# Two more projection blocks cut into token halves at three norm transitions of a two-layer trunk, with their weights split ahead

## The chip, the cores and the metric

One core of a Trainium2 chip (trn2) runs the whole step in one launch. The time is the device time of that launch in microseconds (us). A core has five engines that run beside each other, each with a queue of its own worked off in order, and that wait for one another through semaphores only: PE (TensorE, matmuls), DVE (VectorE), ACT (ScalarE), POOL (GpSimd) and SP (SyncE, which here issues the DMAs). PE writes to PSUM, eight banks of 512 floats on 128 partitions, and ACT and DVE read its results there.

## The reference

The trunk has two layers over 128 context tokens and 512 latent tokens, 1024 features wide. Each layer is a mixer and a gated convolutional FFN; each of the four sub-layers is wrapped in two norms. What lies between two sub-layers is this:

```
def rmsnorm(x, g):
    xf = x.astype(jnp.float32)
    y = xf * lax.rsqrt(jnp.mean(xf * xf, axis=-1, keepdims=True) + EPS)
    return (y * g.astype(jnp.float32)).astype(x.dtype)
...
    h = rmsnorm(x, prm["norm_pre"][l, 0]) * (1.0 + scale1) + shift1
    (mixer: projections of h, attention and/or delta rule, then @ w_out -> mix)
    x = x + gate1 * rmsnorm(mix, prm["norm_post"][l, 0])
    h = rmsnorm(x, prm["norm_pre"][l, 1]) * (1.0 + scale2) + shift2
    f = conv_ffn(h, prm["ffn_w_up"][l], prm["ffn_conv"][l], prm["ffn_w_down"][l])
    x = x + gate2 * rmsnorm(f, prm["norm_post"][l, 1])
...
def conv_ffn(h, w_up, conv_w, w_down):
    u = dwconv_centred(h @ w_up, conv_w)
    a, b = jnp.split(u, 2, axis=-1)
    return (jax.nn.silu(a) * b) @ w_down
```

Layer 0 has the even mixer (attention and delta rule), layer 1 the odd one: `h @ w_in` gives 384 query columns (`cq`), 256 key-value columns (`ckv`) and 64 rotary columns (`kpe`); `cq` and `ckv` are normed again and projected into heads.

## The kernel before

**Tiling.** All activations lie transposed, features on the partitions, as eight chunks of 128 features (`KD` = 8) by 644 token columns (`TW`: 640 tokens and gaps). The columns are cut into two halves of 322 (`HW`, function `tk(g)`). A projection is done in blocks of 128 output columns, numbered through the whole program; `n` is the number, `N0_FFN[l]`, `N0_ODD_IN` and so on are the first of a stage. To reach full precision each operand is split in two fp32r numbers, hi and lo, and a product is three matmuls (hi·hi, hi·lo, lo·hi). A block of eight chunks is thus 8 x 3 x 2 halves = 48 matmuls of 128x322.

**Weights.** SP loads block n into `w_raw[n % 2]` when the lo part of block n-2 is written (`raw_free`). ACT copies it to `w_hi` (`hi`, L782), DVE subtracts to get `w_lo` (`w_rest`, L1338). Both have two buffers. The guard of `hi(n)` before the copy is

```
                if not isinstance(n, int) or n >= 2:
                    act.wait_ge(proj_done, n - 1)
```

and `proj_done` counts finished blocks, so that block n-2 has been read. The output projections have six further weight buffers, `RESH` and `RESL` (named `w_out_hi`, `w_out_lo`), which lie in the space of `g_hi` and `g_lo` and hold output blocks 2 to 7.

**A norm transition.** There are three of them with the same code: i = 0 (even output projection into the up projection of layer 0), i = 1 (down projection of layer 0 into the odd layer's input projection), i = 2 (odd output projection into the up projection of layer 1). While PE still works on half 1 of the projection in front of the norm, ACT and DVE already norm half 0. PE's part is `pair_halves`:

1. half 0 of the first two blocks, n and n+1 (`pair_chunk`, L1997), with the statistics of the norm behind (`post_stat`) among them;
2. `second_stat` (L2034): eight fp32 matmuls of ones with squares of x, which sum them over the features of half 1; each pair waits for a square on ACT (L853);
3. half 1 of blocks n and n+1, chunk by chunk, as `h_lo` of half 1 comes (L1413 on DVE, behind L874 on ACT, L1407 on DVE, and the root on ACT, L841 and L843);
4. then the remaining blocks by `proj` (L1964), both halves at a time.

On ACT and DVE `second_half` is the other side of this: root of the norm behind, four pairs of x (`x_pair`, L1371 and L1373), four squares, root of the norm in front, eight chunks of h. For i = 1 PE also turns the context rows there, and ACT copies them from PSUM (`context`).

**After it.** In the FFN, blocks come in pairs, a and b. For each pair ACT and DVE run a `body`: ACT splits the weights two blocks ahead, evacuates PSUM into `u` and `conv` (L1168, L1169) for a, then the same for b, then silu (L1172), and `g_hi` (L1174); DVE does the lo part, two convolution steps per block (L1797, L1800), the gating (L1808) and `g_lo` (L1810). There are 11 bodies per half of the FFN; the middle ones are a hardware loop. A block uses PSUM banks 0 and 1 or 2 and 3, by n % 2. Banks 4 to 7 are used by the statistics alone. In the odd layer six blocks follow: ACT evacuates three `cq`, two `ckv` and one `kpe` block; PE does the statistic of `cq` (`norm_stat`, L1985) behind block 3 and that of `ckv` behind block 5; the first head projections follow. POOL zeroes the edge columns of `g_hi` and `g_lo`.

## Time and profile before

| | us |
|---|---|
| median of 3 runs | 1990.46 |
| lowest and highest | 1989.63, 1992.21 |
| the profiled execution, its time | 1988.44 |
| its span, first to last instruction | 1986.6 |
| PE busy | 1869.2 (94%) |
| DVE busy, ACT busy | 964.9 (49%), 845.1 (43%) |
| PE's share of the chain that ended last | 86% |
| TensorE clock, mean | 0.982 of full |

The profile is of one execution. Matmuls overlap, so one that is listed with 0.31 us may be issued 0.15 us after the one before it; what counts is the distance of their starts. The fp32 statistics matmuls appear as two records each. The idle time of an engine stands in brackets behind the row that ended it, with what released it. The granted clock is given as a share of 2.4 GHz.

### The profile page before, as it was taken

Reading aid. Unit: us, or ns where it says so; the run is one execution under the profiler, and the core shown is the slowest. Engines: PE = TensorE matmul, PEld = TensorE weight load, DVE = VectorE, ACT = ScalarE, POOL = GpSimd, SP = SyncE. Lnnn points to the kernel's source line nnn. Section 1 sums busy time; section 2 is a strip of 40 time slices with the busy share of each in tenths; the row PEclk is TensorE's granted clock in tenths of the full one; section 3 lists DMA queues with packets and bytes.
Section 4 is the critical chain, followed back from the end, with each engine's and each line's share of the span. In section 5 each row is a group of like instructions: output and inputs, shape, how many; then the busy total and the mean of one; then the engine's idle time right before and its main releaser. Section 6 shows DMA issues by size and latency. Waiting matters only on the chain.

```text
span 1986.6 us, 35678 instructions
## 1 busy us (share of the span) xinstructions
PE 1869.2 (94%) x14484; PEld 1725.9 (87%) x14484; DVE 964.9 (49%) x1558; ACT 845.1 (43%) x1464; POOL 87.9 (4%) x126
## 2 busy tenths in 40 slices
PE   4999999998889999999999999998899999999997
PEld 2999877776779899999999887776798999999997
DVE  4433354445655555325555754344355553255555
ACT  4445322223655544214445644343455442144453
POOL 0000233321000000000000000000000000000000
PEclk8999999999989999999999999999999999999999
DMA  7222454443020122312224311101201223122243
GB/s 276 64 66 57 175 176 168 158 167 115 1 65 25 53 74 78 88 57 74 74 86 132 101 38 48 28 25 43 64 22 56 72 78 88 57 74 74 86 132 112
DMA packets 238715, 170.12 MB, mean 86 GB/s; under 512 B 20138, under 2 KB 230284, under 8 KB 232332
## 3 DMA queue, kind: packets, MB, share of 16 engines
q1 hardware_dynamic: 238604, 168.54, 27.6%
q8 instruction: 82, 1.34, 0.3%
q14 instruction: 29, 0.24, 0.0%
HBM read 165.08 MB, written 3.44 MB: 85 GB/s over the span
## 4 chain that ended last, share of the span: by engine, by line
PE 86%; DVE 5%; ACT 4%; issue 3%; POOL 2%; DMA 0%; SPq 0%; ACTq 0%; DVEq 0%; POOLq 0%
PE ps L1964 48%; PE ps L2040 12%; PE ps L1997 5%; PE ps L2295 4%; PE ps L2145 2%; PE ps L2553 2%; PE ps L2150 2%; PE ps L2590 2%; PE ps L2549 2%; POOL level_b L730 1%; PE ps L2430 1%; PE ps L2407 1%; ACT w_hi L782 1%; PE ps L1985 1%; DVE scores L1762 1%
## 5 line engine op out<-in xcount | busy, mean ns | idle before, releaser
L782 ACT ACTIVATE w_hi<-w_raw 128x1024 fp32r<-128x1024 f32 (+4 forms) x193 | 205.1, 1063 | 580.4 <-PE ps L1964 478.7
L1338 DVE TENSOR_TENSOR w_lo<-w_raw,w_hi 128x1024 fp32r<-128x1024 f32 (+4 forms) x197 | 241.5, 1227 | 394.2 <-ACT w_hi L782 394.0
L1964 PE MATMUL ps<-h_hi,w_hi 128*128 128x322 f32 x1744 | 403.6, 313 | 5.3 <-ACT conv L1169 2.4
L1964 PE MATMUL ps<-h_lo,w_hi 128*128 128x322 f32 x1744 | 402.4, 312 | 0.0
L1964 PE MATMUL ps<-h_hi,w_lo 128*128 128x322 f32 x1744 | 400.1, 310 | 0.0
L1964 PEld LDWEIGHTS ps<-h_hi,w_hi 128*128 128x128 f32 x1744 | 294.2, 189 | 7.2 <-DVE w_lo L1338 3.4
L1964 PEld LDWEIGHTS ps<-h_hi,w_lo 128*128 128x128 f32 x1744 | 295.4, 189 | 0.0
L1964 PEld LDWEIGHTS ps<-h_lo,w_hi 128*128 128x128 f32 x1744 | 295.3, 189 | 0.0
L2040 PE MATMUL ps<-g_hi,w_hi 128*128 128x322 f32 x352 | 110.8, 315 | 2.7 <-DVE g_lo L1810 1.6
L2040 PE MATMUL ps<-g_hi,w_lo 128*128 128x322 f32 x352 | 109.3, 311 | 0.0
L2040 PE MATMUL ps<-g_lo,w_hi 128*128 128x322 f32 x352 | 109.2, 310 | 0.0
L1797 DVE SCALAR_TENSOR_TENSOR conv<-u,vec_cols,conv 128x642 f32<-128x642 f32 x88 | 78.0, 886 | 12.5 <-ACT conv L1169 12.1
L1800 DVE SCALAR_TENSOR_TENSOR conv<-u,vec_cols,conv 128x642 f32<-128x642 f32 x88 | 78.1, 887 | 11.1 <-DVE conv L1797 0.6
L1174 ACT ACTIVATE g_hi<-gated 128x642 f32 (+1 forms) x44 | 32.6, 741 | 104.5 <-DVE gated L1808 104.5
L1014 ACT ACTIVATE level_z<-ps 128x256 f32<-128x256 f32 (+1 forms) x60 | 22.9, 382 | 110.8 <-PE ps L2295 93.8
L2040 PEld LDWEIGHTS ps<-g_hi,w_hi 128*128 128x128 f32 x352 | 66.3, 188 | 4.0 <-DVE g_lo L1810 2.2
L1169 ACT ACTIVATE conv<-ps,vec_cols 128x644 f32<-128x644 f32 x88 | 69.7, 792 | 0.0
L2040 PEld LDWEIGHTS ps<-g_lo,w_hi 128*128 128x128 f32 x352 | 66.4, 189 | 0.2
L2040 PEld LDWEIGHTS ps<-g_hi,w_lo 128*128 128x128 f32 x352 | 66.4, 189 | 0.0
L1824 DVE COPY f_t<-ps 128x644 f32 (+1 forms) x16 | 13.3, 828 | 100.9 <-PE ps L1964 82.3
L1964 PE MATMUL ps<-g_hi,w_lo 128*128 128x322 f32 x264 | 60.8, 312 | 0.0
L1168 ACT ACTIVATE u<-ps 128x644 f32<-128x644 f32 x88 | 60.8, 691 | 0.0
(367 smaller groups left out, 3372.8 us busy)
## 6 DMA issues: line engine op xcount, KB each, us to landing
w_raw<-in_ffn_w_up SPq DMA_DIRECT2D x88, 512.0 KB, 3.6
w_mod_raw<-in_w_mod SPq DMA_DIRECT2D x40, 1024.0 KB, 5.0
w_raw<-in_ffn_w_down SPq DMA_DIRECT2D x48, 704.0 KB, 4.3
w_raw<-in_ev_w_in SPq DMA_DIRECT2D x18, 512.0 KB, 3.6
w_mod_first<-in_w_mod SPq DMA_DIRECT2D x8, 1024.0 KB, 15.7
w_raw<-in_ev_w_out SPq DMA_DIRECT2D x8, 512.0 KB, 3.9
w_raw<-in_od_w_out SPq DMA_DIRECT2D x8, 512.0 KB, 3.8
w_raw<-in_od_w_kv_up SPq DMA_DIRECT2D x24, 128.0 KB, 2.2
```

Of the source, the lines that this page charges most:

```text
L782: act.activation(WH[slot][:, 0:k, :], RAW[slot][:, 0:k, :], ACT.Copy).then_inc(w_hi, 1)
L1168: act.activation(halves(U[b][:, :]), pair(2 * slot), ACT.Copy).then_inc(S("f_u"), 1)
L1169: act.activation(halves(Y[b][:, :]), pair(2 * slot), ACT.Copy, scale=vcol(v0 + b * FCH, j)).then_inc(evac_a, 1)
L1338: dve.tensor_tensor(WL[slot][:, 0:k, :], RAW[slot][:, 0:k, :], WH[slot][:, 0:k, :].bitcast(F32), ALU.subtract).then_inc(w_lo, 1)
L1797: dve.scalar_tensor_tensor(y[:, 1:643], u[:, 0:642], vcol(v0 + b * FCH, j), y[:, 1:643], ALU.mult, ALU.add).then_inc(S(f"f_conv{b}"), 1)
L1800: last = dve.scalar_tensor_tensor(y[:, 1:643], u[:, 2:644], vcol(v0 + b * FCH + 4 * FCH, j), y[:, 1:643], ALU.mult, ALU.add)
L1964: last = pe.matmul(out, w_of(k, wi), x_of(k, xi, i), start=(k == 0 and p == 0), stop=(k == ks - 1 and p == 2))
L1997: last = pe.matmul(bank(2 * slot + hf, HW), (WH, WL)[wi][slot][:, k, :], x[xi][:, k, hf * HW:(hf + 1) * HW], start=(k == 0 and p == 0), st ...
L2040: last = pe.matmul(out, w[wi][:, k, :], x[xi][:, k, tk(g)], start=(k == 0 and p == 0), stop=(k == ks - 1 and p == 2))
L2145: return pe.transpose(out, src, IDENT[0:rows, 0:rows])
L2150: last = pe.matmul(PS[32 * j:32 * j + 32, b * 512:b * 512 + 512], SCX[:, k, :], w[:, 512 * j:512 * j + 512], start=(k == 0), stop=(k == KD ...
L2295: last = pe.matmul(out(b, h), w[half(b), h, :], x(b, h), start=True, stop=True)
```

## The change

At each of the three transitions blocks n+2 and n+3 are now treated like n and n+1, with half 0 before half 1:

- **PE.** Behind `second_stat` comes `second_pair(0)`: half 0 of blocks n+2 and n+3. Behind half 1 of n and n+1 comes `second_pair(1)`: their half 1. Their results go to banks 4 to 7. The loop over the up blocks begins at block 6, with blocks 4 and 5 written out in front of it.
- **Weights.** Blocks n+2 and n+3 are split into `RESH`/`RESL` buffers instead of `w_hi`/`w_lo`: the copy on ACT (`ahead_hi`) behind the root of the norm behind and behind the second square, the subtraction on DVE behind the last `x_pair`. `next_weights` gives the buffers; `res_slot` turns round which output block uses which, so that these two are free in time.
- **Bodies.** In body 0 the weights of blocks n+4 and n+5 are split (`ahead` = 4), by the same `hi` with its guard unchanged; body 1 splits none and reads banks 4 to 7. In the odd layer blocks 0 and 1 split blocks 4 and 5, blocks 2 and 3 none, and the `cq` statistic stands behind block 4, in banks 6 and 7.
- **Edges.** POOL zeroes the edges of `g_hi` and `g_lo` when block n+3 is done, and PE waits for it only in front of the down blocks.

```
+    def res_slot(m):
+
+        return (m + 2) % 6
+
+    def next_weights(i, u):
+
+        x = u + (1 if i % 2 else 2)
+        return RESH[x], RESL[x]
...
-                pool.wait_ge(S("half_done"), 8 * (l + 1))
+                pool.wait_ge(proj_done, N0_FFN[l] + 4)
...
+            def ahead_hi(i, u):
+
+                n = N0_OUT[i] + (2 * KD if i % 2 else KD) + u
+                act.wait_ge(w_landed[n % 2], landed_by(n))
+                if i % 2:
+                    act.wait_ge(proj_done, N0_OUT[i] + 2 * KD)
+                else:
+                    act.wait_ge(S("half_done"), 8 * (i // 2) + 4)
+                act.activation(next_weights(i, u)[0][:, :, :], RAW[n % 2][:, 0:KD, :], ACT.Copy).then_inc(w_hi, 1)
+
             def second_half(i, between=None):
 
                 root(i, "post", 1)
+                ahead_hi(i, 2)
                 for j in range(4):
                     x_square(i, 1, j)
-                    if between and j == 1:
-                        between()
+                    if j == 1:
+                        if between:
+                            between()
+                        ahead_hi(i, 3)
                 root(i, "pre", 1)
...
-                    def body(j, ks):
+                    def body(j, ks, ahead=2, b0=0):
                         c = c0 + j
                         for b in range(2):
                             n = n0 + b + 2 * j
                             slot = (n0 + b) % 2
                             act.wait_ge(proj_done, n + 1)
-                            hi(n + 2, slot=slot, k=ks, landed=landed_by(n0 + b + 2) + 16 * j)
+                            if ahead:
+                                hi(n + ahead, slot=slot, k=ks, landed=landed_by(n0 + b + ahead) + 16 * j)
...
-                    body(0, KD)
-                    with act.Fori(1, FH - 1) as j:
+                    if half == 0:
+                        body(0, KD, 4)
+                        body(1, KD, 0, 4)
+                    else:
+                        body(0, KD)
+                    with act.Fori(2 - half, FH - 1) as j:
...
-                hi(n + 2)
+                if m not in (2, 3):
+                    hi(n + (4 if m < 2 else 2))
...
(DVE, second_half, behind the four x_pair)
+                for u in (2, 3):
+                    n = N0_OUT[i] + (2 * KD if i % 2 else KD) + u
+                    w = next_weights(i, u)
+                    dve.wait_ge(w_hi, n + 1)
+                    dve.tensor_tensor(w[1][:, :, :], RAW[n % 2][:, 0:KD, :], w[0][:, :, :].bitcast(F32), ALU.subtract).then_inc(w_lo, 1)
...
(PE, pair_halves)
                 second_stat(i)
+                if between:
+                    pe.wait_ge(S("c_ctx"), 2)
+
+                def second_pair(g):
+
+                    for u in (2, 3):
+                        pe.wait_ge(w_lo, n + u + 1)
+                        for k in range(KD):
+                            last = half_mm(bank(4 + 2 * ((n + u) % 2) + g, HW), next_weights(i, u), (Hh, Hl), k, g, KD)
+                        if g:
+                            last.then_inc(proj_done, 1)
+                second_pair(0)
...
                 for k in range(KD - 2, KD):
                     pair_chunk(n, 1, k, (Hh, Hl), KD, (1,))
+                second_pair(1)
...
                         pair_halves(n0, 2 * l)
-                        pe.wait_ge(*filled(f"g_edges{l}"))
-                    with pe.Fori(1 - half, FH) as j:
+                        for b in range(2):
+                            proj(n0 + b + 4, H, free=[evacuated(n0 + b)])
+                    with pe.Fori(3 * (1 - half), FH) as j:
...
+                    pe.wait_ge(*filled(f"g_edges{l}"))
                     down_pair(n1, FH * (2 * l + half))
...
-            for m in range(2, 6):
-                proj(N0_ODD_IN + m, H)
-                if m == 3:
-                    norm_stat("cq")
+            for m in range(4, 6):
+                proj(N0_ODD_IN + m, H, free=[evacuated(N0_ODD_IN + m - 4)])
+                if m == 4:
+                    norm_stat("cq", 6)
```

The order of instructions shows it at three places of the first transition. In brackets stand the semaphores an instruction waits for.

PE, from the last two statistics matmuls on, before: half 1 of block 0 with `w_hi1`, chunk by chunk behind `h_lo`.

```order
L2034 MATMUL ps<-x_sq1_85,consts_61 128x322 [waits x_squared]
L2034 MATMUL ps<-x_sq1_85,consts_61 128x322
L1997 MATMUL ps<-h_hi_50,w_hi1_58 128x322 [waits h_lo,half_evacuated]
L1997 MATMUL ps<-h_lo_51,w_hi1_58 128x322
L1997 MATMUL ps<-h_hi_50,w_lo1_60 128x322
L1997 MATMUL ps<-h_hi_50,w_hi1_58 128x322 [waits h_lo]
```

And after: half 0 of block 2, with weights from an output buffer (`w_out_hi4`), waits for its own weights alone.

```order
L2071 MATMUL ps<-x_sq1_85,consts_61 128x322 [waits x_squared]
L2071 MATMUL ps<-x_sq1_85,consts_61 128x322
L2077 MATMUL ps<-h_hi_50,w_out_hi4_98 128x322 [waits w_lo_written]
L2077 MATMUL ps<-h_lo_51,w_out_hi4_98 128x322
L2077 MATMUL ps<-h_hi_50,w_out_lo4_104 128x322
L2077 MATMUL ps<-h_hi_50,w_out_hi4_98 128x322
```

48 such matmuls, with `w_out_hi4` and then `w_out_hi5`, have come between the statistics and the first wait for `h_lo` of half 1.

ACT, from the root of the norm behind (`post_rstd`) to that of the norm in front (`pre_rstd`), before:

```order
L843 ACTIVATE post_rstd_93<-post_rstd_93 128x322 [waits norm_root]
L853 ACTIVATE x_sq0_84<-x_t_49 128x644 [waits x_added]
L853 ACTIVATE x_sq1_85<-x_t_49 128x644 [waits x_added]
L853 ACTIVATE x_sq0_84<-x_t_49 128x644 [waits x_stat,x_added]
L853 ACTIVATE x_sq1_85<-x_t_49 128x644 [waits x_stat,x_added]
L841 ACTIVATE pre_rstd_92<-ps,eps_73 128x322 [waits h_scaled,x_stat]
```

And after:

```order
L852 ACTIVATE post_rstd_93<-post_rstd_93 128x322 [waits norm_root]
L894 ACTIVATE w_out_hi4_98<-w_raw1_56 128x1024 [waits half_done,w_landed1]
L862 ACTIVATE x_sq0_84<-x_t_49 128x644 [waits x_added]
L862 ACTIVATE x_sq1_85<-x_t_49 128x644 [waits x_added]
L894 ACTIVATE w_out_hi5_99<-w_raw0_55 128x1024 [waits half_done,w_landed0]
L862 ACTIVATE x_sq0_84<-x_t_49 128x644 [waits x_stat,x_added]
L862 ACTIVATE x_sq1_85<-x_t_49 128x644 [waits x_stat,x_added]
L850 ACTIVATE pre_rstd_92<-ps,eps_73 128x322 [waits h_scaled,x_stat]
```

One weight copy has come in front of the first square and one in front of the third.

ACT, from the silu of body 0 to the first weight copy in the loop, before (that copy is for block 4):

```order
L1172 ACTIVATE silu_a_116<-conv0_114 128x642 [waits f_conv0]
L1174 ACTIVATE g_hi_52<-gated_117 128x642 [waits f_gated]
L1177 UNCONDITIONAL_BRANCH
L1177 ISA
L779 ISA [waits proj_done]
L782 ACTIVATE w_hi1_58<-w_raw1_56 128x1024 [waits proj_done,w_landed1]
```

And after (the copy is for block 6):

```order
L1195 ACTIVATE silu_a_116<-conv0_114 128x642 [waits f_conv0]
L1197 ACTIVATE g_hi_52<-gated_117 128x642 [waits f_gated]
L1191 ACTIVATE u0_112<-ps 128x644 [waits f_silu,f_gated,f_conv0,proj_done]
L1192 ACTIVATE conv0_114<-ps,vec_cols_62 128x644
L1191 ACTIVATE u1_113<-ps 128x644 [waits f_silu,f_gated,f_conv1,proj_done]
L1192 ACTIVATE conv1_115<-ps,vec_cols_62 128x644
L1195 ACTIVATE silu_a_116<-conv0_114 128x642 [waits f_conv0]
L1197 ACTIVATE g_hi_52<-gated_117 128x642 [waits f_gated]
L1204 UNCONDITIONAL_BRANCH
L1204 ISA
L788 ISA [waits proj_done]
L791 ACTIVATE w_hi1_58<-w_raw1_56 128x1024 [waits proj_done,w_landed1]
```

Body 1, four evacuations, a silu and a `g_hi`, now stands in front of the loop and has no weight copies.

## Rows read from the trace of the kernel before

**Rows 1.** The page: busy time by engine; a weight load (KB, us to landing).

```profile
PE 1869.2 (94%) x14484; PEld 1725.9 (87%) x14484; DVE 964.9 (49%) x1558; ACT 845.1 (43%) x1464; POOL 87.9 (4%) x126
...
w_raw<-in_ffn_w_up SPq DMA_DIRECT2D x88, 512.0 KB, 3.6
```

**Rows 2.** Timeline of PE, first transition: start us, us, operation, count, [idle before <-releaser].

```profile
643.54 4.88 PE L2034 MATMUL ps<-x_sq,consts 128*128 128x322 f32 x16
...
651.41 0.61 PE L1997 MATMUL ps<-h_hi,w_hi 128*128 128x322 f32 x1 [2.98 <-DVE h_lo L1413]
...
657.34 0.31 PE L1997 MATMUL ps<-h_hi,w_hi 128*128 128x322 f32 x1
...
661.23 0.31 PE L1997 MATMUL ps<-h_hi,w_lo 128*128 128x322 f32 x1
662.77 0.56 PE L1964 MATMUL ps<-h_hi,w_hi 128*128 128x322 f32 x2 [1.23 <-ACT conv L1169]
...
691.49 0.46 PE L1964 MATMUL ps<-h_hi,w_hi 128*128 128x322 f32 x2
```

**Rows 3.** PE by stretches, first transition: stretch, us, busy (count), PEclk, DMA share, GB/s.

```profile
648.00:649.00 1.00, 0.42 (x2) 1.00 0.00 0
...
651.00:652.00 1.00, 0.59 (x2) 0.50 0.00 0
```

**Rows 4.** Timeline of ACT, from the first transition's statistics into the up blocks.

```profile
641.47 0.74 ACT L853 ACTIVATE x_sq<-x_t 128x644 f32<-128x644 f32 x1 [1.76 <-DVE x_t L1373]
...
644.88 0.74 ACT L853 ACTIVATE x_sq<-x_t 128x644 f32<-128x644 f32 x1 [1.06 <-PE ps L2034]
...
662.54 1.06 ACT L782 ACTIVATE w_hi<-w_raw 128x1024 fp32r<-128x1024 f32 x1
...
668.32 0.74 ACT L1174 ACTIVATE g_hi<-gated 128x642 fp32r<-128x642 f32 x1 [1.38 <-DVE gated L1808]
...
677.50 1.06 ACT L782 ACTIVATE w_hi<-w_raw 128x1024 fp32r<-128x1024 f32 x1 [4.82 <-PE ps L1964]
...
679.05 0.79 ACT L1169 ACTIVATE conv<-ps,vec_cols 128x644 f32<-128x644 f32 x1
...
682.91 0.74 ACT L1174 ACTIVATE g_hi<-gated 128x642 f32 x1 [2.44 <-DVE gated L1808]
```

**Rows 5.** Timeline of DVE, same stretch.

```profile
645.42 0.83 DVE L1373 TENSOR_TENSOR x_t<-x_t,f_t 128x644 f32<-128x644 f32 x1
649.53 1.01 DVE L1407 SCALAR_TENSOR_TENSOR h_chunk<-x_t,pre_gain,pre_rstd 128x320 f32<-128x320 f32 x2 [3.28 <-ACT pre_rstd L843]
...
656.97 0.55 DVE L1413 SCALAR_TENSOR_TENSOR h_lo<-h_chunk,mod,h_hi 128x320 fp32r<-128x320 f32 x1 [0.16 <-ACT h_hi L874]
```

**Rows 6.** Timeline of PE, transition into the odd layer.

```profile
1140.30 1.35 PE L2034 MATMUL ps<-x_sq,consts 128*128 128x322 f32 x4 [0.25 <-ACT x_sq L853]
...
1169.56 1.25 PE L1985 MATMUL ps<-sq_sum,consts 128*128 128x322 f32 x4
...
1184.94 1.25 PE L1985 MATMUL ps<-sq_sum,consts 128*128 128x322 f32 x4
1185.78 0.71 PE L1964 MATMUL ps<-cq_hi,w_hi 128*128 128x322 f32 x2
```

**Rows 7.** Odd layer: DVE at 1128.66 and 1180.47, ACT at 1175.51 and 1178.06.

```profile
1128.66 1.23 DVE L1338 TENSOR_TENSOR w_lo<-w_raw,w_hi 128x1024 fp32r<-128x1024 f32 x1 [1.27 <-ACT w_hi L782]
...
1175.51 0.74 ACT L1243 ACTIVATE cq_hi<-cq 128x644 fp32r<-128x644 f32 x1
1178.06 0.53 ACT L782 ACTIVATE w_hi<-w_raw 128x384 fp32r<-128x384 f32 x1 [1.80 <-PE ps L1964]
...
1180.47 0.83 DVE L1349 TENSOR_TENSOR sq_sum<-sq_sum,sq 128x644 f32<-128x644 f32 x1
```

**Rows 8.** Timeline of PE, third transition.

```profile
1487.48 4.89 PE L2034 MATMUL ps<-x_sq,consts 128*128 128x322 f32 x16
...
1506.34 0.56 PE L1964 MATMUL ps<-h_hi,w_hi 128*128 128x322 f32 x2 [1.22 <-ACT conv L1169]
```

44 lines of the change are left out of this document (24 added, 20 removed).

## The prediction

> **What bounds the kernel now.** I read the page first, then the timelines of PE, ACT and DVE around the three places where a norm lies between two projections. PE is busy for 94% of the span [rows 1], so a gain can only come from a stretch in which PE stands idle or runs at the lower clock. The transitions are such stretches. Take the first, into the up projections of layer 0. Eight statistics matmuls (16 records) start at 643.54 and the last one leaves PE at about 648.25 (the run of 4.88 us less what the last matmul overlaps, 0.17). Then PE is idle for 2.98 us until the first `h_lo` chunk of token half 1 [rows 2]. The granted clock, still 1.00 (2.4 GHz) at 648 to 649, is 0.50 (1.2 GHz) at 651 to 652 [rows 3], so the 22 matmuls between 651.41 and 657.34 come every 0.27 us. From 657.34 they come at full rate, and the pair of blocks is issued at 661.38 (one step after the row at 661.23). Then PE waits again, until 662.77, for ACT's evacuation and the split of the next weights. Full rate is read from 662.77 to 691.49: four blocks of 48 matmuls in 28.72 us, 0.150 us each, **7.18 us a block** [rows 2]. In the rest I number the blocks after the norm 0 to 6; 691.49 is the start of block 6.
>
> **Part 1: matmuls that move.** PE now runs half 0 of blocks 2 and 3 (48 matmuls, 7.2 us) between the statistics and half 1 of blocks 0 and 1, and their half 1 behind it. No matmul is added: 48 and 48 take the place of 96. Each of them keeps one weight load, as before (matmuls and loads have equal counts in [rows 1]). What the move covers at the first transition: idle 651.41 - 648.25 = 3.16 us; half 1 of blocks 0 and 1 took 661.38 - 651.41 = 9.97 us where 7.18 is enough, 2.79 us of low clock and of waits for chunks; the gap 662.77 - 661.38 = 1.39 us, since block 2's weights and banks are now ready ahead. Sum 7.3 us. Half 1 now starts at 648.25 + 0.25 + 7.18 = 655.7 (0.25 us is a guess for the first matmul behind statistics). The first `h_lo` chunk is there at 651.3 and the eighth at 657.5 [rows 2, 5], 0.9 us apart; PE wants the eighth only at 655.7 + 0.45 x 2 + 0.9 x 5 = 661.1, and each earlier one late enough too. No wait there.
>
> **Part 2: weight splits that move.** Two ACT copies and two DVE subtractions per transition go ahead, in the order shown above. ACT's first copy (1.06 us, the price of the row at 662.54) falls into the 1.76 us in which ACT waits for DVE before the first square, at 641.47. The second stands in front of the third square, which began at 644.88 after 1.06 us of idleness: a copy of 1.06 us just fits [rows 4]. Cost 0 for both. DVE's two subtractions (1.23 us each [rows 7]) start when its last `x_t` is done, 646.25, and end at 648.7; its next work starts at 649.53 after 3.28 us of idleness [rows 5]. PE needs the first at 648.25 (done 647.5) and the second at 651.9. Cost 0, with 0.8 us to spare on DVE. If that cover were gone, half 1 would still have 655.7 - 651.3 = 4.4 us before PE noticed. In the odd layer ACT also copies the context there, and the copy delays the third square by some 0.5 us; PE sees 0.1 us of it. The weights of the second copy can only be loaded after the split that ends at 1129.89 [rows 7]; they are needed 7.5 us later, and such a load lands 3.6 us after its issue [rows 1]. The four edge memsets on POOL now wait for block 3, and PE's wait for them stands 140 us later, in front of the down blocks: cost 0.
>
> **Part 3: what is late next.** The split of block 4 keeps its old guard, `proj_done >= n - 1`, and that now means that block 2 is done, though block 4 only overwrites the buffer of block 0. Behind this copy in ACT's queue stand the evacuations of blocks 0 and 1 and both bodies of the gated convolution. By PE's count: blocks 0 and 1 end at 662.9, block 2 at 666.5, block 3 at 670.1, block 4 at 677.2, block 5 at 684.4. ACT starts the copy for block 4 at 666.5 and has evacuated block 0 2.34 us later (677.50 to 679.84 [rows 4]), 668.9, so block 4 (from 670.1) does not wait. The copy for block 5 starts at 670.1. Before, body 0 took 6.5 us from that copy to the end of `g_hi` (662.54 to 669.06); I take 6.2, since DVE is less behind: 676.3. Body 1 has no copies: two evacuations of 1.37 us, and 3.8 us from the last evacuation to `g_hi` (679.84 to 683.65), and 0.4 us because two blocks' convolutions now fall together on DVE: 683.2. Only then comes the copy for block 6, inside the loop, at 683.3, and 2.34 us later, with semaphores 685.8, PE may start block 6, which it wants at 684.4. **A new wait of 1.4 us.** Its bounds are 0 (body 1 a quarter faster) and 2.7 us (1.28 us more for entering the loop, the idle time of ACT at that place before, which hides it). The loop cannot stay late: ACT needs 2.34 + 6.15 (677.50 to 683.65) = 8.5 us a body, and PE 14.4.
>
> Gain at the **first transition**: before, 648.25 to 691.49 = 43.24 us; after, 0.25 + 5 x 7.18 + 1.4 = 37.55; **5.7 us**. At the **third** the statistics start 843.94 us later and block 2 843.57 us later [rows 2, 8], so before loses 0.37 us less: **5.3 us**.
>
> **Odd layer.** Before, the statistics leave PE at 1141.5 and the first query projection starts at 1185.78: 44.3 us. After: 0.1 + 0.25 + five blocks 35.9 + the `cq` statistic 0.84 (1184.94 to 1185.78 is the price [rows 6]) = PE stands at the `ckv` statistic at 1178.6. The `cq` statistic itself hardly moves: it stood at 1169.56, two blocks before the end, and will stand at 1170.4, one block before the end. The chain behind it ends with `cq_hi` at 1176.25 [rows 7]; I shift it by 0.4 us, between 0 (ACT was late then) and 0.84. Behind it follow the copy, the evacuation, two squares and their sum, 1178.06 to 1181.30 = 3.24 us [rows 7], which before fitted under block 5. Now they end at 1176.65 + 3.24 = 1179.9. PE waits 1.3 us, and the query projection starts at 1180.8. Gain **5.0 us**, not the 6.3 that the moved blocks save.
>
> **Sum.** 5.7 + 5.0 + 5.3 = 16.0 us. The profiled execution took 1988.44 us, so 1972.4; the median of the three runs is 2.02 us above it, 1990.46, so **1974.5 us**, 0.8% less. About 0.2%, 4 us, is what a measurement of this kernel can tell from no change.
>
> **Rival 1: the clock falls all the same.** PE no longer idles for 3 us, but in the statistics it still waits for squares in short gaps (0.25 us in [rows 6]; in the first transition PE's 4.88 us for eight matmuls hold some too), and then come dense matmuls. If the clock falls at each transition for as many matmuls as before, it costs 22 x (0.27 - 0.15) = 2.6 us each, 7.9 in all: 1982.4 us. Against it: at 648 to 649, with the statistics just over, the clock is 1.00 [rows 3], and it is lower only where PE has been idle. The Trainium skill, "TensorE: Matmul & The Clock Gate", section "A second HAM failure mode: psum-queue depth-cycling", speaks for the rival: short idle spells between groups of matmuls can be enough to make the clock swing between its two levels. By that rule the time would be the 1982.4 above; this trace does not show it. Chance 8%.
>
> **Rival 2: the waits of part 3 are larger.** Each at its upper end (2.7, 2.7, and 2.6 if body and sums run late by another 1.3), gain 12.1 us: 1978.4. Chance 13%. **Rival 3: they vanish**, gain 20.1: 1970.4. Chance 8%; it needs ACT and DVE both to run their chains faster than the rows show.
>
> **Rival 4: slower.** The up loops stay one body late. This decides where ACT's chain of a body passes PE's 14.4 us: each us above costs 9 bodies x 2 loops = 18 us, so 15.5 us a body would give 1974.5 + 20 = 1994. At 8.5 us a body it is far off; the second copy waiting for its weights decides likewise only from 7.5 + 4.4 us of loading. Chance 2%. **Rival 5: nothing moves**, because the second pair waits for its splits on PE until the chunks are there anyway (DVE 3 us late at every transition): PE would be idle as before, and keep only the gap, 1.39 x 3 less the new waits of 4.1: 1990. Chance 3%.
>
> **Chances.** Forecast 66% (gain 13 to 19), rivals 8, 13, 8, 2 and 3%. The range runs from rival 3 to rival 1, 1970 to 1982, and leaves out some 15%. Faster by over 0.2%: 94%; within: 3%; slower: 3%.
>
> **What would show it.** On PE: at 648.3 `w_out_hi` matmuls of half 0 directly behind the statistics, no idle time for `h_lo`, PEclk 1.00 through all three transitions; a new wait of 1 to 2 us for block 6 at two places, released by ACT's evacuation or DVE's `w_lo`, and one for `sq_sum` of about 1.3 us in front of the `ckv` statistic. On ACT: the copy for block 4 begins when block 2 ends. I am wrong if the clock is below 1.00 behind the statistics, if half 1 waits for chunks, or if a wait for `w_lo` stands in front of the second pair.

## The result, and the profile after

The changed kernel takes 1973.95 us (median of four runs, 1970.57 to 1978.02), the kernel before 1991.34 us in the same comparison (four runs, 1989.63 to 1994.39): a ratio of 0.9912, with a 95% interval of 0.9889 to 0.9935. It is **17.4 us faster**; 16.0 were forecast, and the forecast time was 1974.5 us. The profiled execution took 1974.58 us with a span of 1972.8, against 1988.44 and 1986.6 before.

The first transition on TensorE (PE), the answer to [rows 2]: start us, us, engine, line, operation, shapes, count, and in brackets the idle time before it and what ended it.

```profile
645.52 4.91 PE L2071 MATMUL ps<-x_sq,consts 128*128 128x322 f32 x16
650.03 0.55 PE L2077 MATMUL ps<-h_hi,w_out_hi 128*128 128x322 f32 x1
650.42 0.31 PE L2077 MATMUL ps<-h_lo,w_out_hi 128*128 128x322 f32 x1
...
657.39 0.31 PE L2034 MATMUL ps<-h_hi,w_hi 128*128 128x322 f32 x1
...
671.73 0.47 PE L2001 MATMUL ps<-h_hi,w_hi 128*128 128x322 f32 x2
...
685.73 0.46 PE L2001 MATMUL ps<-h_hi,w_lo 128*128 128x322 f32 x2
686.94 0.56 PE L2001 MATMUL ps<-h_hi,w_hi 128*128 128x322 f32 x2 [0.75 <-ACT conv L1192]
```

The `w_out_hi` matmuls are the first halves of blocks 2 and 3. They stand where 2.98 us of idle time stood; 657.39 is the start of half 1, 671.73 of block 4, 686.94 of block 6. Neither half 1 nor block 4 has a bracket: nothing waits for `h_lo` or for a weight split. Block 6 could have started one step (0.29 us) behind the row at 685.73, at 686.02, so the new wait is 0.92 us. From the first statistics matmul to block 6 it is 686.94 - 645.52 = 41.42 us, against 691.49 - 643.54 = 47.95 before [rows 2]: **6.53 us less**.

The granted clock in stretches of 1 us, the answer to [rows 3] (stretch, us, busy time and matmuls, then PE's clock as a share of 2.4 GHz, DMA share, GB/s). The first two rows stand in the first transition, the last two behind the statistics of the others:

```profile
651.00:652.00 1.00, 1.00 (x9) 1.00 1.00 284
657.00:658.00 1.00, 1.00 (x9) 1.00 0.08 16
```

```profile
1144.00:1145.00 1.00, 1.00 (x9) 1.00 0.00 0
...
1490.00:1491.00 1.00, 1.00 (x9) 1.00 0.00 0
```

ScalarE (ACT) in the same stretch, the answer to [rows 4]: both weight copies, the third square directly behind the second of them, the copies for blocks 4 and 5 (668.42 and 672.01), the end of body 0 (677.30) and of body 1 (683.85), and the copy for block 6 (684.49).

```profile
641.62 1.05 ACT L894 ACTIVATE w_out_hi<-w_raw 128x1024 fp32r<-128x1024 f32 x1
...
645.72 1.04 ACT L894 ACTIVATE w_out_hi<-w_raw 128x1024 fp32r<-128x1024 f32 x1
646.86 0.74 ACT L862 ACTIVATE x_sq<-x_t 128x644 f32<-128x644 f32 x1
...
668.42 1.06 ACT L791 ACTIVATE w_hi<-w_raw 128x1024 fp32r<-128x1024 f32 x1 [9.45 <-PE ps L2077]
...
672.01 1.06 ACT L791 ACTIVATE w_hi<-w_raw 128x1024 fp32r<-128x1024 f32 x1 [1.24 <-PE ps L2077]
...
677.30 0.74 ACT L1197 ACTIVATE g_hi<-gated 128x642 fp32r<-128x642 f32 x1 [0.90 <-DVE gated L1842]
...
683.85 0.74 ACT L1197 ACTIVATE g_hi<-gated 128x642 fp32r<-128x642 f32 x1 [1.90 <-DVE gated L1842]
684.49 1.05 ACT L791 ACTIVATE w_hi<-w_raw 128x1024 fp32r<-128x1024 f32 x1
```

VectorE (DVE), the answer to [rows 5]. The two subtractions (2.35 us together) have shrunk the idle time in front of the first chunk of half 1 from 3.28 to 1.02 us:

```profile
648.17 2.35 DVE L1434 TENSOR_TENSOR w_out_lo<-w_raw,w_out_hi 128x1024 fp32r<-128x1024 f32 x2
651.54 1.01 DVE L1440 SCALAR_TENSOR_TENSOR h_chunk<-x_t,pre_gain,pre_rstd 128x320 f32<-128x320 f32 x2 [1.02 <-ACT pre_rstd L852]
```

PE in the odd layer and at the third transition, the answers to [rows 6] and [rows 8]:

```profile
1133.85 4.82 PE L2071 MATMUL ps<-x_sq,consts 128*128 128x322 f32 x16
...
1176.58 1.35 PE L2022 MATMUL ps<-sq_sum,consts 128*128 128x322 f32 x4 [1.11 <-DVE sq_sum L1377]
1177.53 0.71 PE L2001 MATMUL ps<-cq_hi,w_hi 128*128 128x322 f32 x2
...
1479.22 4.90 PE L2071 MATMUL ps<-x_sq,consts 128*128 128x322 f32 x16
...
1520.64 0.56 PE L2001 MATMUL ps<-h_hi,w_hi 128*128 128x322 f32 x2 [0.74 <-ACT conv L1192]
```

From the statistics to the query projection it is 43.68 us (49.33 before), a gain of 5.65; at the third transition 41.42 us (47.57 before, block 6 at 1535.05), a gain of 6.15. **The three gains add up to 18.3 us**; compared like with like it is 18.0, as the next experiment shows. The spans differ by 13.8 us and the medians by 17.4, so the whole has to be read with care. The first statistics matmul of the first transition comes at 645.52 us in this profile and at 643.54 in the one before, although everything ahead of it is the same program. From that matmul to the end of the span it is 1327.3 us, before 1343.1. In what follows I use two measures that the stretch ahead doesn't enter: the **three lengths** (statistics to block 6, to the query projection, to block 6) and the **rest**, the span less the start of the first statistics matmul.

### The profile page after: what moved, and what is told of

It reads as the page before. It is cut to its first block, busy times and chain, and to the rows that moved or that the text cites. A ratio compares the mean times of both kernels' runs of the same rounds, so it can differ in the third digit from the quotient of the medians.

```text
span 1972.8 us, 35612 instructions
## 1 busy us (share of the span) xinstructions
PE 1870.9 (95%) x14484; PEld 1728.6 (88%) x14484; DVE 961.2 (49%) x1558; ACT 845.8 (43%) x1464; POOL 87.1 (4%) x126
## 3 DMA queue, kind: packets, MB, share of 16 engines
q8 instruction: 85, 1.39, 0.3%
## 4 chain that ended last, share of the span: by engine, by line
PE 85%; DVE 6%; ACT 4%; issue 3%; DMA 1%; SPq 0%; POOL 0%; ACTq 0%; DVEq 0%; POOLq 0%
PE ps L2001 45%; PE ps L2077 14%; PE ps L2345 4%; PE ps L2034 4%; PE ps L2195 3%; PE ps L2605 2%; PE ps L2200 2%; PE ps L2642 2%; PE ps L2601 2%; PE ps L2480 1%; PE ps L2457 1%; ACT w_hi L791 1%; PE ps L2022 1%; DVE scores L1795 1%; DVE w_lo L1366 1%
## 5 line engine op out<-in xcount | busy, mean ns | idle before, releaser
L2001 PE MATMUL ps<-h_hi,w_hi 128*128 128x322 f32 x1648 | 381.4, 313 | 3.2 <-ACT conv L981 1.7
L2001 PE MATMUL ps<-h_lo,w_hi 128*128 128x322 f32 x1648 | 380.2, 312 | 0.0
L2001 PE MATMUL ps<-h_hi,w_lo 128*128 128x322 f32 x1648 | 378.0, 310 | 0.0
L2001 PEld LDWEIGHTS ps<-h_hi,w_hi 128*128 128x128 f32 x1648 | 278.1, 189 | 4.8 <-ACT conv L1192 2.0
L2001 PEld LDWEIGHTS ps<-h_hi,w_lo 128*128 128x128 f32 x1648 | 279.1, 189 | 0.0
L2001 PEld LDWEIGHTS ps<-h_lo,w_hi 128*128 128x128 f32 x1648 | 279.0, 189 | 0.0
L2077 PE MATMUL ps<-g_hi,w_lo 128*128 128x322 f32 x352 | 109.1, 310 | 0.0
L2077 PE MATMUL ps<-h_hi,w_out_hi 128*128 128x322 f32 x288 | 90.8, 315 | 0.0
L2077 PE MATMUL ps<-h_lo,w_out_hi 128*128 128x322 f32 x288 | 89.8, 312 | 0.0
L2077 PE MATMUL ps<-h_hi,w_out_lo 128*128 128x322 f32 x288 | 89.5, 311 | 0.0
L1192 ACT ACTIVATE conv<-ps,vec_cols 128x644 f32<-128x644 f32 x88 | 69.7, 792 | 0.0
```

Of the source, the lines that this page charges most:

```text
L1192: act.activation(halves(Y[b][:, :]), pair(b0 + 2 * slot), ACT.Copy, scale=vcol(v0 + b * FCH, j)).then_inc(evac_a, 1)
L2001: last = pe.matmul(out, w_of(k, wi), x_of(k, xi, i), start=(k == 0 and p == 0), stop=(k == ks - 1 and p == 2))
L2077: last = pe.matmul(out, w[wi][:, k, :], x[xi][:, k, tk(g)], start=(k == 0 and p == 0), stop=(k == ks - 1 and p == 2))
```

## Experiments

### The changed kernel again

No edit. 

> The changed kernel once more, beside the others of this call, as their base. Every theory expects what the first comparison gave: a ratio near 0.991 to the kernel before, that is about 17 us less. Read from its profile: from the first statistics matmul of the first transition to the first matmul of block 6 in 41.4 us (47.95 before), of the third in 41.4 us (47.57 before), and from the odd layer's statistics to the query projection in 43.7 us (49.33 before). If these three lengths come back within 0.2 us while the whole time moves by 2 us or more, then the scatter of the whole time sits outside the transitions, in the stretches with a lowered clock.

Measured: 1973.91 us, ratio 0.9914 (0.9883 to 0.9945); in a later comparison 1972.72 us, ratio 0.9902 (0.9884 to 0.9921). Lengths 41.38, 44.02 and 41.40 us, and 41.41, 44.05 and 41.38 us. The rest is 1324.6 and then 1324.7 us, **18.5 us less than before**, which is the sum of the lengths' gains (18.0) within the reading. In the first profile the rest is 2.7 us longer, with two stretches of low clock that these two lack (at 1126 and 1208 us). For the second:

> The changed kernel once more, as the base of this call's others. Every theory expects a ratio of 0.991 and the lengths of c1_after (41.4, 44.0 and 41.4 us) within 0.1 us; the low-clock stretches before 640 us take other places or another number than in c1_after, and that moves the whole time by some 2 us.

So the lengths of the even transitions repeat within 0.05 us. The odd one has two values, 43.68 us in the first profile and 44.02 or 44.05 here, and the traces say why. In the first profile the clock had dropped ahead of that transition, behind a wait of 2.22 us (last section), TensorE came 1.5 us later to the statistics, and all squares stood ready: 4.82 us for the statistics, without a wait. In the two profiles here it did not drop, and the statistics wait for the third square (the view ends within this run of matmuls):

```profile
1135.31 2.00 PE L2071 MATMUL ps<-x_sq,consts 128*128 128x322 f32 x6 [0.32 <-ACT x_sq L862]
```

In the profile of the kernel before the clock did not drop there either (wait of 0.25 us, [rows 6]). So its 49.33 us belong beside 44.0, the gain of the odd transition is 5.3 us and not 5.65, and **the three together are 18.0 us**. In what follows an odd length is compared with 43.68 where the clock dropped ahead of it, and with 44.0 where it didn't.

The first statistics matmul came at 645.02 and 645.82 us here, and between 643.54 and 651.36 us in all thirteen profiles, though the program ahead of it is the same in each. That spread of 7.8 us, and such stretches behind it, make single runs scatter; the transitions add 0.4 us at most. The clock of that stretch differs too, between 0.95 and 0.97 of full speed over the first 640 us, but it does not order the starts: four profiles with the same mean of 0.952 there start at 645.92, 647.91, 648.72 and 651.36, and the two with the lowest, 0.949, at 645.52 and 645.55. What makes the rest of the spread stays open.

### The clock alone

```
 second_stat(i)
+for x in range(20):
+    pe.matmul(bank(4, HW), WH[n % 2][:, x % 6, :], Hh[:, x % 6, tk(0)],
+              start=(x == 0), stop=(x == 19))
```

This is the kernel before; only these matmuls are added. 

> The kernel before with 20 further matmuls behind the statistics of each of the three transitions, on operands that are there already, written to a bank that nobody reads at that time: they add nothing to the output. They take 3.0 us at the full clock, in which TensorE stood idle for 2.98 us. Theory (part of the gain came from the clock, which drops behind the idle time): the granted clock stays at 1.00 behind the statistics in all three transitions, the chunks of half 1 run at 0.15 us a matmul, and each transition is about 2.0 us shorter (45.9 us from statistics to block 6 in place of 47.95), up to 0.7 us of the 2.79 staying as waits for h_lo: in all 6 us less, ratio 0.997. Rival (the matmuls of half 1 were slow because their operands came late, not because of the clock): the clock stays up but the transition is no shorter, 47.9 us, ratio 1.000. Second rival (the clock falls all the same, since a matmul that does no useful work counts the same as idle time): neither clock nor length changes.

Measured: 1987.77 us, ratio 0.9975 (0.9958 to 0.9992), 4.4 us less. The filler between the statistics and half 1, the first chunks of half 1, and the clock there:

```profile
649.61 1.59 PE L2083 MATMUL ps<-h_hi,w_hi 128*128 128x322 f32 x8
...
653.00 0.39 PE L1997 MATMUL ps<-h_hi,w_hi 128*128 128x322 f32 x1
...
653.84 0.42 PE L1997 MATMUL ps<-h_hi,w_hi 128*128 128x322 f32 x1 [0.15 <-DVE h_lo L1413]
```

```profile
651.00:652.00 1.00, 1.00 (x9) 1.00 0.00 0
654.00:655.00 1.00, 0.79 (x4) 1.00 0.00 0
```

The clock stays at 1.00, and the chunks of half 1 come in time with short waits for `h_lo` (0.15 to 0.21 us, five of them in the three transitions). From the statistics to block 2 it is 662.65 - 645.13 = 17.52 us, against 662.77 - 643.54 = 19.23 before: 1.7 us less. At the third it is 1.3 us (18.86 and 17.52). The odd length is 47.78 us, 1.55 less than before, but in this profile the clock had dropped ahead of it (at 1129.94 us) and the statistics had no wait; from the end of the statistics on it is 43.20 us against 44.13, 0.9 less. That makes 4.0 us in all, and the whole time, with its interval of 1.6 to 8.4 us less, agrees. The theory of the clock holds, with a size of 0.9 to 1.7 us a transition in place of 2.0. Both rivals fall. So of the 18.0 us **some 4.0 are the clock**: they were to be had without moving any useful work. What remains of the 2.79 us that the prediction counted in half 1 are waits for chunks, 1.1 us at the first transition.

### One transition undone

```
+if i != 1:
     second_pair(0)
...
+if i != 1:
     second_pair(1)
-for m in range(4, 6):
-    proj(N0_ODD_IN + m, H, free=[evacuated(N0_ODD_IN + m - 4)])
-    if m == 4:
-        norm_stat("cq", 6)
+for m in range(2, 6):
+    proj(N0_ODD_IN + m, H)
+    if m == 3:
+        norm_stat("cq")
```

The splits on ACT and DVE are undone in the same way. 

> The changed kernel with the odd layer's transition as it was before: blocks 2 and 3 there are projected whole behind half 1, their weights split after it; the two even transitions keep the change. Theory (the three transitions are independent, and each gives its own gain): the odd transition goes back to 49.3 us from 43.7, the other two stay at 41.4; the whole is 5.6 us above the changed kernel, ratio to before about 0.994. Rival (the gain of one transition changes what follows, since the clock or the loads of the next stretch depend on when it comes): the length at the odd transition goes back by 5.6 us but the whole moves by something else, under 3 or over 8 us, with the rest found in another stretch of the profile.

Measured: 1979.64 us, ratio 0.9940 (0.9918 to 0.9962), 5.7 us above the changed kernel of the same comparison. Lengths 41.41, **48.80** and 41.40 us. The old idle time is back at the one place:

```profile
1139.36 0.61 PE L2036 MATMUL ps<-h_hi,w_hi 128*128 128x322 f32 x1 [2.98 <-DVE h_lo L1447]
...
1149.36 0.56 PE L2003 MATMUL ps<-h_hi,w_hi 128*128 128x322 f32 x2 [1.14 <-DVE w_lo L1367]
```

The odd length goes back by 4.8 us, the others don't move. The kernel before has 49.33 us there, 0.5 more. This half microsecond stands between the start of half 1 and block 2: 10.00 us here, 10.51 before. The low clock, as long in both, began 0.35 us ahead of half 1 here, partly over idle time, and 0.79 us behind its start before. The rest is 6.5 us longer than in the changed kernel; 1.7 us of the difference is a stretch of low clock at 1210 to 1215 us, which the changed kernel's profile of that comparison doesn't have. The transitions are independent, as the sum in the prediction assumed.

### The guard

```
-def hi(n, slot=None, k=None, landed=None):
+def hi(n, slot=None, k=None, landed=None, back=2):
 ...
-        act.wait_ge(proj_done, n - 1)
+        act.wait_ge(proj_done, n + 1 - back)
```

`back` is 4 for the copies of blocks 4 and 5. 

> The changed kernel, with the wait on the copies for blocks 4 and 5 relaxed: the copy for block 4 waits for block 0 alone (its raw tile's earlier reader) and no longer for block 2. Theory (the guard makes the wait): the copy for block 4 is ready some 10 us earlier, ScalarE starts the evacuation and the copy for block 6 earlier, and the wait of 0.92 us in front of block 6 goes at both even transitions, so each takes 40.5 us from statistics to block 6 in place of 41.4; the query path keeps its 1.1 us in front of the ckv statistic, since that one hangs on the square sums. In all 1.8 us less than the changed kernel, ratio to before about 0.990. Rival (the wait belongs to the chain of evacuation, convolution and copy on ScalarE, whatever the guard): block 6 still waits 0.9 us, and no length changes by more than 0.2 us. A second rival: the copy made early stands in the way of squares or roots on ScalarE, and a statistics matmul or a chunk of half 1 waits by up to 1 us instead.

Measured: 1970.99 us, ratio 0.9892 (0.9864 to 0.9921). ACT, and PE at block 6:

```profile
662.39 1.06 ACT L791 ACTIVATE w_hi<-w_raw 128x1024 fp32r<-128x1024 f32 x1 [4.54 <-PE ps L2034]
...
664.63 1.06 ACT L791 ACTIVATE w_hi<-w_raw 128x1024 fp32r<-128x1024 f32 x1
...
678.11 1.06 ACT L791 ACTIVATE w_hi<-w_raw 128x1024 fp32r<-128x1024 f32 x1 [0.42 <-PE ps L2001]
```

```profile
684.93 0.46 PE L2001 MATMUL ps<-h_hi,w_hi 128*128 128x322 f32 x2
```

The two copies now go at the end of blocks 0 and 1 (662.39 and 664.63), the copy for block 6 is done more than 5 us before PE wants it, and block 6 follows without a gap. Lengths 40.49, 44.04 and 40.51 us: 0.9 us less at each even transition, nothing at the odd one. The wait of part 3 is the guard's and not that of the chain. The query path keeps its wait, `[1.11 <-DVE sq_sum L1377]`. The median is 2.9 us below the changed kernel's, but the rest is 1324.5 us, only 0.1 less, since this profile has one more stretch of low clock (1.7 us lost, at 1204 to 1208 us). The whole time can't resolve 1.8 us; the lengths can.

### How much room has half 1?

```
+for x in range(3):     # 9 in the second kernel
+    step(dve.tensor_tensor(TNP[0][:, :, :], both_k(X, 0, 1),
+                           two(RSTP), ALU.mult))
 l, s = SUB[i + 1]
 dve.wait_ge(*root_ready(i, "pre", 1))
```

> The changed kernel with three more products of 644 columns on VectorE in each transition, behind the two weight splits and ahead of the first chunk of half 1; they are written to a scratch pair and add nothing to the output. One takes 0.83 us (about 0.9 with its wait), so 2.8 us, of which 1.0 fill the wait for the root that stood there: the chunks of half 1 come 1.8 us later. Theory (the projected blocks 2 and 3 leave VectorE some 3.3 us of room, at the chunk that is nearest to being late): nothing is seen, 41.4 us from statistics to block 6, 44.0 to the query projection, ratio 0.991. Rival (the splits have used up the room: VectorE is the bound of half 1): each transition is 1.8 us longer, 5.4 in all, ratio 0.994.

Measured: 1974.07 us, ratio 0.9909 (0.9885 to 0.9933), lengths 41.41, 44.05 and 41.43 us: nothing is seen, although the chunks come 1.5 us later against the statistics (658.86 - 651.36 = 7.50 us to the first, 5.99 in the changed kernel). VectorE is not the bound of half 1.

> The same with nine such products, 8.3 us: the chunks of half 1 come 7.3 us later. Theory (3.3 us of room): TensorE stands idle for 4.0 us in front of half 1 at each transition, and the clock falls there as it did in the kernel before, for a further 1.6 us: 45.4 us from statistics to block 6 with the clock up, 47.0 with it down, so 12 to 17 us in all, ratio 0.997 to 1.000. Rival (what is late on VectorE is absorbed by the waits of blocks 6 and the query path): 42.5 us, ratio 0.993. Rival without room: 48.7 us, ratio 1.002.

Measured: 1988.42 us, ratio 0.9989 (0.9978 to 1.0000); lengths **46.55, 47.62 and 46.06 us**. DVE and PE at the first transition, and the clock:

```profile
658.22 1.01 DVE L1442 SCALAR_TENSOR_TENSOR h_chunk<-x_t,pre_gain,pre_rstd 128x320 f32<-128x320 f32 x2
```

```profile
660.10 0.39 PE L2036 MATMUL ps<-h_hi,w_hi 128*128 128x322 f32 x1 [2.51 <-DVE h_lo L1448]
```

```profile
661.00:662.00 1.00, 0.78 (x4) 0.97 0.00 0
662.00:663.00 1.00, 1.00 (x4) 0.50 0.00 0
```

The first chunk starts 658.22 - 645.55 = 12.67 us behind the first statistics matmul, in the changed kernel 651.01 - 645.02 = 5.99. It is 6.68 us late. PE waits for 2.51 us by the bracket, and half 1 starts 2.68 us later than in the changed kernel (14.55 us behind the first statistics matmul, 11.87 there): **the room is 4.0 to 4.2 us**. The prediction had 4.4; my 3.3 of the expectation was too small. It went by the third chunk, but when the first chunk is late, PE also wants the third one later. With that room the idle time comes out at 2.5 in place of 4.0, and behind it the clock falls as forecast (1.7 us lost at each of the three). The kernel is then hardly faster than the one before: late chunks and the clock together take back 13.8 us of the 18.0 (the odd length against 43.68, since the clock dropped ahead of it here too).

### Is ScalarE free?

```
 ahead_hi(i, 3)
+for x in range(2):
+    act.activation(TNP[x][:, :, :], both_k(X, 0, 1), ACT.Copy)
```

> The changed kernel with two more copies of 0.74 us on ScalarE behind the second weight copy, ahead of the third square of half 1; they are written to a scratch pair and add nothing to the output. Theory (the squares and with them the statistics are on the path, and ScalarE has 0.7 us of idle time between the third and the fourth square at the even transitions, none at the odd one): the last square is 0.8 us late at the even transitions and 1.4 us at the odd one, and TensorE waits for just that between the statistics: 42.2, 45.4 and 42.2 us, 3.0 us in all, ratio 0.993. Rival (the projection ahead takes this up, as it takes up the chain behind the squares): no length changes by more than 0.2 us; it would be wrong to call the splits free only because of their place.

Measured: 1975.29 us, ratio 0.9913 (0.9890 to 0.9936); lengths **42.16, 44.92 and 42.15 us**, 0.8, 1.2 and 0.8 us more than in the changed kernel (the clock dropped ahead of the odd transition here, so 43.68 is its base). PE between the statistics of the first and of the odd transition:

```profile
649.11 2.44 PE L2073 MATMUL ps<-x_sq,consts 128*128 128x322 f32 x8 [0.86 <-ACT x_sq L862]
...
1138.73 2.44 PE L2073 MATMUL ps<-x_sq,consts 128*128 128x322 f32 x8 [1.30 <-ACT x_sq L862]
```

At the even transitions it is as expected: the square that is 0.8 us late is paid in full, and the projection behind it takes up nothing. At the odd one I expected 1.4 us and found 1.2: in the changed kernel's profile with the same drop, PE had no wait in these statistics and ACT was idle for 0.1 us in front of the fourth square; now PE waits for 1.30 us. So the two weight copies of the change are free **only because each lies in idle time of ACT**, and little of it is left: of some 1.5 us more on ACT ahead of the third square, 0.8 us are paid at the even transitions and 1.2 at the odd one. The whole-time ratio can't show this: 2.8 us stand in the lengths, and the spread is as large.

### Is all of the cover needed?

```
-second_pair(0)
+second_pair(0, (2,))
 (half 1 of blocks 0 and 1)
-second_pair(1)
+second_pair(1, (2,))
+second_pair(0, (3,))
+second_pair(1, (3,))
```

> The changed kernel with block 2 alone projected between the statistics and half 1; both halves of block 3 follow behind half 1, in the order block 2 second half, block 3 first half, block 3 second half. The cover is 3.6 us in place of 7.2. Theory (what has to be covered ends with the first chunk of h_lo, which stood ready 4.1 us before TensorE wanted it in c1_after): half 1 begins 3.6 us sooner, its first chunk is in time by 0.5 us, its third chunk is 0.4 us late and a later one about 0.1, so half 1 takes some 0.6 us more; the clock stays at 1.00. Block 2 is done 3.6 us sooner, so that the guard lets the copy for block 4 go sooner and the wait of 0.92 us in front of block 6 goes as in e1_guard. Even transitions 41.4 + 0.6 - 0.9 = 41.1 us, the odd one 44.0 + 0.6 = 44.6 us, the whole within 0.5 us of the changed kernel, ratio 0.991. Rival (the full cover is needed, since the pace of VectorE, 0.93 us a chunk, is slower than TensorE's 0.89 and gaps keep coming back, with the clock falling behind them): 43 to 44 us at the even and 46 us at the odd transition, ratio 0.994.

Measured: 1976.66 us, ratio 0.9920 (0.9900 to 0.9940); lengths **42.08, 44.34 and 42.07 us**. Half 1 starts sooner, at 657.01, which is 8.29 us behind the first statistics matmul and not 11.87, and one chunk is late:

```profile
657.01 0.31 PE L2034 MATMUL ps<-h_hi,w_hi 128*128 128x322 f32 x1
...
658.36 0.41 PE L2034 MATMUL ps<-h_hi,w_hi 128*128 128x322 f32 x1 [0.22 <-DVE h_lo L1446]
```

Block 4 starts 0.7 us later than in the changed kernel (26.88 against 26.18 us) at the even transitions, and the odd length is 0.7 us above 43.68, its base here, since the clock dropped ahead of it; the expectation had 0.6. The clock is 1.00 throughout (658 to 659 us: 1.00 with PE busy for 0.78). So a cover of 3.6 us brings all but 0.7 us a transition, and the rival falls. The whole was forecast within 0.5 us of the changed kernel, and its median is 3.9 us above: 2.0 us stand in the lengths, and this profile has two stretches of low clock more (at 1130 and 1212 us). My second number was wrong: the wait in front of block 6 should have gone with the earlier end of block 2, and it is there unchanged (`[0.74 <-ACT conv L1192]`). ACT tells why:

```profile
668.73 1.06 ACT L791 ACTIVATE w_hi<-w_raw 128x1024 fp32r<-128x1024 f32 x1 [6.58 <-PE ps L2077]
...
675.88 1.06 ACT L791 ACTIVATE w_hi<-w_raw 128x1024 fp32r<-128x1024 f32 x1 [4.82 <-PE ps L2077]
```

The copy for block 4 does go sooner (20.0 us behind the statistics in place of 22.9), but then ACT waits for 4.82 us at the copy for block 5, which is released by the end of **block 3**. That copy starts 27.2 us behind the statistics (26.5 in the changed kernel), 0.7 us later, like block 4 and block 6. Of the two guards the second one makes the wait. The guard experiment relaxed both, and so couldn't tell.

### A candidate that takes the remaining waits

```
 act.wait_ge(proj_done, n + 1 - back)         # as in the guard experiment
 ...
(PE, block 4 of the odd layer, in place of its proj)
+for k in range(KD):
+    pair_chunk(n, 0, k, H, KD)
+    if k == 6:
+        norm_stat("cq", 6)
 ...
-if g and (m, k) == (0, 2):                   # second FFN projection
+if g and (m, k) == (0, 5):
     post_stat(i, 0)
```

> A candidate: the changed kernel with the guard relaxed as in e1_guard, the odd layer's query statistic moved from behind block 4 to behind seven of its eight chunks, and the statistic of the first half of the second FFN projection behind the sixth chunk of its block in place of the third. Theory: the 0.9 us in front of block 6 is gone (twice, shown by e1_guard); the statistic comes 0.9 us sooner, its root and the query's scaling too, so the wait in front of the ckv statistic falls from 1.1 to 0.2 us; the waits of 0.68 us for the last square of the FFN output go (twice). In all 1.8 + 0.9 + 1.4 = 4.1 us less than the changed kernel, ratio about 0.989. Rival (ScalarE, not the statistic, holds the ckv squares, or the later statistic makes the residual sums late and moves the wait to the next statistic): the query path stays at 44.0 us, the squares' wait comes back behind, and only 1.8 us are left, ratio 0.990.

Measured: 1972.44 us, ratio 0.9908 (0.9886 to 0.9931). Then once more, with more runs and beside the changed kernel:

> e7_all once more, with more rounds and beside the changed kernel: its first comparison could not tell it from the changed kernel (ratios 0.9908 and 0.9909 to 0.9914), although its lengths were 40.5, 42.8 and 40.5 us and two waits of 0.68 us were gone. Theory (the gains add up, and the whole time of the first comparison was moved by the low-clock stretches outside): 1.8 + 1.2 + 1.4 = 4.4 us less than c2_after in the median, ratio 0.989. Rival (what is saved there is given back in front of the next wait, and the whole is no shorter): the same ratio as c2_after within 0.0005.

Measured: **1970.64 us, ratio 0.9889** (0.9870 to 0.9908), against 1972.72 us and 0.9902 for the changed kernel. Lengths 40.5, 42.8 and 40.5 us in both runs. PE at the `ckv` statistic, and two rows of its waits (us in all, times, longest):

```profile
1176.30 1.35 PE L2022 MATMUL ps<-sq_sum,consts 128*128 128x322 f32 x4 [0.16 <-DVE sq_sum L1377]
```

```profile
PE ps L2056 <- ACT f_sq L829: 3.4, 2, 2.2
PE ps L2022 <- DVE sq_sum L1377: 0.9, 2, 0.7
```

In the changed kernel the first row was 4.8 us in four waits: the two of 0.68 us are gone. Of the two waits in the second row one is that of the `ckv` statistic, which fell from 1.11 to 0.16 us; the other lies ahead of the transitions, in layer 0, and is between 0.7 and 1.6 us in the profiles of either kernel. The clock dropped ahead of the odd transition in both profiles, so 42.8 us belong beside 43.68, 0.9 less. Each of the three parts does what was expected of it: 1.8 + 0.9 + 1.4 = 4.1 us in the trace. Of the whole time 2.1 us are seen in the medians, and the intervals overlap: both profiles have two stretches of low clock more than the changed kernel's in these comparisons (1124 to 1128 and 1206 to 1209 us, 1.7 us each), the rest is 1322.2 and 1322.3 us, 2.4 less. The candidate is the shortest in its parts; that it is faster as a whole than the changed kernel with the guard relaxed (1970.99 us) isn't shown.

## Why the prediction was right, step by step

**Part 1 holds, in mechanism and size.** It counted 3.16 us of idle time, 2.79 of low clock and chunk waits and a gap of 1.39 us, 7.3 in all. No wait for `h_lo`, no gap in front of block 2 or 4, and a clock of 1.00 are what the rows show; the filler kernel splits the 2.79 us into 1.7 of clock and 1.1 of waits. Two prices were a little high: half 1 starts 657.39 - 650.26 = 7.13 us behind the end of the statistics in place of 7.43, in which 0.25 us was a guess, and a block took 7.15 us (671.73 to 686.02 for two) in place of 7.18. From the end of the statistics to the moment at which PE wants block 6 it was 35.76 us where 36.15 had been summed: 0.4 us more gain.

**Part 2 holds.** The splits cost nothing: PE spends 4.74 us in the statistics of the first transition (4.71 before). The 4.4 us of room were 4.0 to 4.2, and the claim that the copies fit into ACT's idle time is right, but with little to spare, as the two extra copies showed (0.8 to 1.2 us paid for 1.5 added).

**Part 3 was right in kind and 0.5 us too large.** A wait of 1.4 us was forecast in front of block 6, 0.92 was found, twice. Counted from the end of the statistics: the copy for block 4 was forecast at 18.25 us and came at 18.16; body 0 ended at 28.05 by the forecast and at 27.8 in the trace; body 1 at 34.95, and in the trace at 34.3 (684.59). Block 6 starts 0.9 us sooner than summed, and PE wants it 0.4 us sooner. The largest term that was mis-sized is body 1: its two evacuations, silu and gating took 6.55 us, not 6.9, so that the 0.4 us added for convolutions that fall together on DVE was too much. From the end of body 1 to block 6 it was 2.35 us, not 2.6, and from the copy for block 5 to the end of body 0 6.0, not 6.2. That it is the guard was argued in the prediction and is now shown. The prediction's text dwells on the copy for block 4, but its sum goes through the copy for block 5, held until block 3 ends, and the kernel with half the cover shows that this is the one that counts. In the odd layer 1.3 us of wait were forecast, 1.11 found.

**The sum.** 5.7, 5.0 and 5.3 us were forecast; the gains in the lengths are 6.5, 5.3 and 6.15 us. Errors: 0.4 us of rate and 0.5 us of wait at each even transition, 0.2 us of wait and 0.1 of rate at the odd one. The lengths alone would have made it 18.0 us and 1972.5; the median of 17.4 lies between that and the 16.0 forecast, and the first measurement is no finer than some 4 us.

**Rivals.** Rival 1, that the clock falls all the same, is refuted by the clock rows of all three transitions, in three profiles of this kernel. The Trainium skill, "TensorE: Matmul & The Clock Gate", section "A second HAM failure mode: psum-queue depth-cycling", says that short idle spells between groups of matmuls can make the clock swing. In these runs idle spells of 0.3 us between the statistics left it at 1.00, and so did 0.86 and 1.30 us in the kernel with two copies more (1139 to 1142 us); the rule doesn't show in the transitions at that length. It may show elsewhere: in two of the thirteen profiles, those of the kernel before (at 1418 us) and of the one with two copies more (at 1413 us), the clock dropped behind a row of short waits, none above 1.39 us and three of them within 4 us. In the kernel with two copies more:

```profile
1412.00:1414.00 2.00, 1.91 (x9) 0.72 0.00 0
1414.00:1416.00 2.00, 2.00 (x9) 0.50 0.04 8
```

Rival 2 and rival 3 bracketed the waits, and these came out between the forecast and rival 3. Rival 4 asked for loops that stay late: the loop catches up, since no further wait for `conv` stands in the rows. Rival 5 is out by the `w_out_hi` row at 650.03.

## What to carry to other kernels

Work that is ready belongs in the stretch in which a norm's chain runs, and it needs to cover only the time to the first chunk: here half of what was moved brought all but 0.7 us a transition. A part of such a gain can be the clock rather than the idle time; a few useless matmuls in the gap measure how much, and are a fallback where nothing useful is ready. When blocks are moved, look at every wait that was written in terms of their order: a guard that was free before, because it named the block just ended, can become the last wait left. And a length between two instructions can depend on what lies ahead of it: a late start hides waits, so compare profiles that start alike.

## What the hardware showed that was not expected

The same idle time doesn't always do the same to the clock. In front of the statistic of the FFN output in the odd transition PE waits for 2.22 us in all thirteen profiles, and the clock drops behind it in seven of them and stays in six. The changed kernel shows both, in two executions. The first:

```profile
1126.00:1127.00 1.00, 1.00 (x5) 0.54 0.06 18
1127.00:1128.00 1.00, 1.00 (x5) 0.50 0.67 152
```

and the second:

```profile
1126.00:1127.00 1.00, 1.00 (x9) 1.00 0.34 59
1127.00:1128.00 1.00, 1.00 (x9) 1.00 0.99 292
```

Behind it the statistics of the odd transition come 8.84 us later in the one and 7.34 us later in the other: 1.5 us for one such drop, of which the statistics give back some 0.35, since they no longer wait for a square. Of the longer waits of this kind, 2.98 us, all four in the profiles of the kernel before and of the undone transition were followed by a drop, and so were the two of 2.51 and 2.53 us in the kernel with nine products more; of the waits of up to 1.30 us in the transitions none was, and one of 1.43 us (nine products more, odd transition) was. The length of the wait alone does not order them: outside the transitions one of 2.08 us (for `c_probs`, at about 1370 us) was followed by a drop in all thirteen profiles, and one of 1.79 us (for `q_rope`, at about 1207 us) in six. So a change that removes such a wait takes away a chance of a loss too, which a single profile can't price. What decides it in the middle stays open; no experiment here varied the wait alone.
